# The recurrence's values brought to tokens on partitions by block transposes and on-chip transfers, and forget tiles projected ahead of them

## What is computed

```python
h = rmsnorm(x, mix_norm_g)
aq, ak, av, hq, hff, hfb, hi, hg, ga, gb = split_columns(h @ w_in)
y_attn = axial_gqa_attention(aq, ak, av, ...) @ w_branch_attn
y_hgrn = hgrn2_bidirectional(hq, hff, hfb, hi, hg, ...) @ w_branch_hgrn
# in the recurrence, per head, in chunks of tokens:
vh = heads(i, HGRN_VAL_DIM)                  # values, from the columns hi
contrib = einsum('bhnsd,bhnse->bhnde', k * exp(b_last - b), v)
o_intra = einsum('bhnts,bhnse->bhnte', scores, v)
```

## Time and profile before

| | |
|---|---|
| time, median of 3 runs | 1134.91 us (1134.86 to 1134.94) |
| the profiled execution | 1135.17 us |
| its span in the trace | 1133.4 us |
| PE busy | 1124.8 us, 99% |
| DVE busy | 628.1 us, 55% |
| ACT busy | 443.8 us, 39% |
| POOL busy | 83.3 us, 7% |
| granted PE clock | 0.998 |
| projection stage, PE units 9 to 25 | about 424 to 550 us of the span |

### The profile page before, as it was taken

The page is one execution under the profiler, slowest core; times in us unless marked ns, Lnnn a source line. Parts: engine busy times, 40 slices in busy tenths (PEclk is TensorE's granted clock), DMA queues, the critical chain, the costliest instruction groups (busy, mean ns, idle before and its releaser), DMA issues.

```text
span 1133.4 us, 16606 instructions
## 1 busy us (share of the span) xinstructions
PE 1124.8 (99%) x6359; PEld 911.9 (80%) x6359; DVE 628.1 (55%) x832; ACT 443.8 (39%) x658; POOL 83.3 (7%) x74
## 2 busy tenths in 40 slices
PE   9999999999999999999999999999999999999997
PEld 7888888888888777776788888888888888888886
DVE  6755555563333596646688767656555555542223
ACT  6423232232222544546856655544232323331223
POOL 0000000000000130000143320020000000000000
PEclk9999999999999999999999999999999999999999
DMA  6332322333322434212221212422243333332221
GB/s 199 122 111 77 108 93 93 117 104 102 102 95 74 177 109 129 75 57 84 69 92 56 71 51 92 177 96 93 79 125 120 89 121 107 119 112 93 99 88 75
DMA packets 51650, 114.78 MB, mean 101 GB/s; under 512 B 21904, under 2 KB 25104, under 8 KB 51344
## 3 DMA queue, kind: packets, MB, share of 16 engines
q1 hardware_dynamic: 32752, 105.16, 27.9%
q10 hardware_dynamic: 18848, 8.92, 2.8%
HBM read 105.41 MB, written 4.19 MB: 97 GB/s over the span
## 4 chain that ended last, share of the span: by engine, by line
PE 98%; DMA 1%; DVE 1%; ACT 0%; ACTq 0%; issue 0%; DVEq 0%
PE ps L1195 27%; PE ps L1197 27%; PE ps L1196 27%; PE ps L1221 4%; PE ps L1220 4%; PE ps L1222 4%; PE ps L1321 1%; PE ps L1338 1%; PE ps L1467 1%; PE ps L1443 1%; DMA xT<-xT_dram 0%; PE ps L1460 0%; PE ps L1421 0%; PE ps L1370 0%; DMA raw<-up_dram 0%; PE ps L1410 0%
## 5 line engine op out<-in xcount | busy, mean ns | idle before, releaser
L1195 PE MATMUL ps<-h_hi,w_hi 128*128 128x512 f32 x1024 | 407.2, 398 | 0.3 <-DVE w_lo L781 0.3
L1197 PE MATMUL ps<-h_hi,w_lo 128*128 128x512 f32 x1024 | 399.1, 390 | 0.0
L1196 PE MATMUL ps<-h_lo,w_hi 128*128 128x512 f32 x1024 | 398.7, 389 | 0.0
L781 DVE TENSOR_TENSOR w_lo<-raw,w_hi 128x1024 fp32r<-128x1024 f32 (+2 forms) x190 | 233.3, 1230 | 176.9 <-ACT w_hi L432 171.0
L432 ACT ACTIVATE w_hi<-raw 128x1024 fp32r<-128x1024 f32 (+1 forms) x182 | 194.7, 1080 | 183.8 <-PE ps L1197 71.6
L1195 PEld LDWEIGHTS ps<-h_hi,w_hi 128*128 128x128 f32 x1024 | 192.2, 188 | 55.6 <-issue 15.2
L1196 PEld LDWEIGHTS ps<-h_lo,w_hi 128*128 128x128 f32 x1024 | 192.3, 188 | 41.8 <-issue 2.9
L1197 PEld LDWEIGHTS ps<-h_hi,w_lo 128*128 128x128 f32 x1024 | 192.2, 188 | 40.4
L504 ACT ACTIVATE g_hi<-un 128x512 fp32r<-128x512 f32 (+1 forms) x44 | 27.8, 632 | 219.5 <-DVE un L781 219.5
L781 DVE TENSOR_TENSOR un<-ps,rs 128x512 f32<-128x512 f32 x44 | 30.4, 691 | 97.3 <-PE ps L1197 97.3
L1195 PE MATMUL ps<-g_hi,w_hi 128*128 128x512 f32 x176 | 68.5, 389 | 0.0
(11 more groups left out here) (232 smaller groups left out, 1151.7 us busy)
## 6 DMA issues: line engine op xcount, KB each, us to landing
raw<-up_dram SPq DMA_DIRECT2D x86, 512.0 KB, 3.3
raw<-proj_dram SPq DMA_DIRECT2D x26, 512.0 KB, 3.4
raw<-down_dram SPq DMA_DIRECT2D x16, 704.0 KB, 4.0
raw<-down_dram SPq DMA_DIRECT2D x22, 512.0 KB, 3.2
raw<-gates_dram SPq DMA_DIRECT2D x16, 512.0 KB, 3.3
raw<-branch_dram SPq DMA_DIRECT2D x8, 512.0 KB, 3.3
raw<-wout_dram SPq DMA_DIRECT2D x8, 512.0 KB, 3.2
x_spill_dram<-xT ACTq DMA_DIRECT2D x1, 2048.0 KB, 7.1
```

Source lines behind the costliest of these rows:

```text
L781: return V.tensor_tensor(out, a, b, op)
L1195: T.matmul(ps[:, bank, :], w_hi[:, slot, cols], moving_hi(j), start=start and j == 0, stop=False)
L1196: T.matmul(ps[:, bank, :], w_hi[:, slot, cols], moving_lo(j), start=False, stop=False)
L1197: ins = T.matmul(ps[:, bank, :], w_lo[:, slot, cols], moving_hi(j), start=False, stop=stop and j == tiles - 1)
```

## The change

The four value tiles of the recurrence no longer go through PE and ACT. In the list the first four forget tiles now come at items 6 to 9 and the value tiles at items 10 to 13. After DVE has copied a value tile into `v_tmp`, it transposes it in place in blocks of 32x32. SP then moves the blocks to their partitions with 16 transfers per tile (32 partitions, four pieces of 32 words each), issued before the loads of units 15, 16, 17 and 18, behind the `v_rep` transfers where these stand too. There is one `v_tmp`, so DVE waits before each further value tile until all transfers of the tile before it have landed (`vh_loaded`). The tile `av` for attention keeps its way through PE and ACT. The diff shows the list, SP ahead of the load of unit i, ACT's copy, DVE's item i, and on PE the waits of the first weighted sum and of the first contributions.

```diff
-PROJ = ([("av", 0), ("ak", 0)] + [("aq", t) for t in range(4)] + [("hi", t) for t in range(4)]
-        + [("hf", h) for h in range(4)] + [("hq", t) for t in range(4)]
+PROJ = ([("av", 0), ("ak", 0)] + [("aq", t) for t in range(4)] + [("hf", h) for h in range(4)]
+        + [("hi", t) for t in range(4)] + [("hq", t) for t in range(4)]
         + [("hf", h) for h in range(4, HH)] + [("hg", t) for t in range(4)])
-V_TILES = {i: w for w, i in enumerate(i for i, (kind, _) in enumerate(PROJ) if kind in ("av", "hi"))}
+V_TILES = {0: 0}
+HI_AT = PROJ.index(("hi", 0))
+HI_SEND = 5
...
+                        if 0 <= i - HI_AT - HI_SEND < 4:
+                            w = i - HI_AT - HI_SEND
+                            sp.wait_ge(vblk_done, w + 1)
+                            blocks = v_tmp[:].rearrange("p (t j c) -> p t j c", j=QUADS, c=BLOCK)
+                            for quad in range(QUADS):
+                                for to in range(QUADS):
+                                    sp.dma_start(v_h[BLOCK * to:BLOCK * (to + 1), :, P * w + BLOCK * quad:P * w + BLOCK * (quad + 1)],
+                                                 blocks[BLOCK * quad:BLOCK * (quad + 1), :, to, :]).then_inc(vh_loaded, 16)
                         sp.wait_ge(lo_done, BASE[name] + i + 1)
...
-                    A(v_a[:] if w == 0 else v_h[:, :, P * (w - 1):P * w], vt, ACT.Copy).then_inc(vn_done, 1)
+                    A(v_a[:], vt, ACT.Copy).then_inc(vn_done, 1)
...
-                w = V_TILES.get(i)
-                if w:
-                    dve.wait_ge(vt_done, w)
+                if kind == "hi":
+                    dve.wait_ge(*((vh_loaded, 16 * QUADS * QUADS * t) if t else (vt_done, 1)))
...
+                if kind == "hi":
+                    dve.wait_ge(proj_read, i + 1 + BANK_CREDIT)
+                    V.transpose(v_tmp[:], v_tmp[:]).then_inc(vblk_done, 1)
                 attention_step(i - FIRST_ITEM)
...
-                    pe.wait_ge(vn_done, 5)
+                    pe.wait_ge(vn_done, 1)
...
-                    pe.wait_ge(vn_done, 5)
+                    pe.wait_ge(vh_loaded, 16 * QUADS * QUADS * 4)
```

More of the change, by code:

```diff
@@ L215, in build @@
         vt_done, vn_done = sem("vt_done"), sem("vn_done")
+        vblk_done, vh_loaded = sem("vblk_done"), sem("vh_loaded")
         qsq_done, qms_done, qeps_done, qr_done = sem("qsq_done"), sem("qms_done"), sem("qeps_done"), sem("qr_done")
```

## The result

| | before | changed kernel |
|---|---|---|
| median time | 1134.93 us (4 runs, 1134.86 to 1135.34) | 1161.80 us (4 runs, 1160.60 to 1162.23) |
| profiled execution | 1135.17 us | 1160.60 us |
| its span | 1133.4 us | 1158.8 us |

The ratio is 1.0231 with a 95% interval from 1.0219 to 1.0243: slower by 2.3%, 26.9 us. The forecast was 1159.1 us, between 1154.5 and 1167.0.

What follows compares the result with a forecast made beforehand. PE's instruction stream was taken to bound the kernel, with SP's added issues deciding: 1135.2 us + 21.7 lateness + 2.5 slow clock = 1159.4, less 0.3 to the median, 1159.1 us; range 1154.5 to 1167 us.

Steps and rivals of the forecast that it cites:

- What bounds the kernel: Whole kernel: PE's instruction stream, busy 99% of the span; work removed gains its full cost, added waits are lost in full.
- The chain: Projection stage: SP's issues delay transfers, DVE's copies, ACT's exponentials, then PE's scores; 21.7 us late at `scores(5)`.
- Bounding the unseen transfer by its neighbours: SP's new issues, a shape not in the trace: 0.633 us each, from similar transfers at 0.59 to 0.63; landing 1.9 us.
- the rival with landings of 4.2 us: Second and third tiles' transfers land late, two such cost 4.6 us more: 1163.7 us and up; 10 in 100.
- The stands: PE waits before `scores(3)`, `scores(4)` and `scores(5)`, ended by ACT's exponentials: 8.4, 9.1 and 6.1 us.
- The clock term: After PE's last stand: eleven matmuls at 0.46 instead of 0.24 us, as at the kernel's start; 2.5 us, bounds 0 and 3.5.
- Late loads alone: Without DVE's wait, unit 18's load issues about 488.7 and `scores(7)` is 17 us late: 1154 us with slow clock.
- The load of unit 18 "just fits": After the fourth tile's issues: its split and exponentials end about 499.0, `scores(7)` is due at 499.1; nothing later is late.
- The rival that the issues do not bind: SP's issues in the stage all hide, needing a pitch of 0.07 us; 1.8 us gained, 1133.1 us; 5 in 100.

Runs made afterwards that it cites:

- the second trace of the changed kernel: The changed kernel, unaltered, run again beside the shortened version with useless matmuls in PE's stands: 1161.27 us, ratio 1.0229.
- the kernel with the later crowds: Against the changed kernel: four value-tile buffers, and the four groups of sixteen issues moved ahead of the loads of units 17 to 20; 1140.44 us, ratio 1.0046.
- the padded kernels: The changed kernel plus useless matmuls before the three late scores: 36, 40, 24 gave 1160.71 us; 36, 28, 16 gave 1159.38 us.
- the spread one: Against the changed kernel: four value-tile buffers, and the 64 issues placed eight ahead of each load of units 17 to 24; 1133.30 us, ratio 0.9981.

## Why the prediction was right, point by point

**What bounds the kernel: right.** Work off PE was worth its full cost once nothing made it wait (1133.30 and 1133.26 us), and every late exponential was paid in full.

**The chain: right in every link, short by 1.6 us at `scores(5)`.** On the time scale of the traces:

| step | forecast | measured |
|---|---|---|
| SP begins the first sixteen issues | 441.4 | 441.87 |
| second tile copied | 452.8 | 453.38 |
| `scores(3)` | 457.0 | 457.62 |
| third tile copied | 468.6 | 469.99 |
| `scores(4)` | 472.8 | 474.23 |
| fourth tile copied | 481.4 | 482.94 |
| `scores(5)` | 485.6 | 487.18 |
| late there | 21.7 | 23.3 |
| added behind the last stand | 2.5, all of it the clock | 2.2, of it 1.5 the clock |
| span | 1157.6 | 1158.8 |

The mis-sized term is the pitch of SP's issues. It was taken as 0.633 us; sixteen took 10.24 us, 0.64 each, which makes 0.3 us over 46 issues. And one issue of the second tile took twice as long (10.84 us for its sixteen), and the start was 0.5 us late, since the first eight `v_rep` took 6.52 us and not 5.96. The rows before already showed such long issues (0.925 us at most); I read them as an exception and left them out of the sum. Whether they are also what the runs differ by is not shown, since only the profiled run of each kernel has a trace. The forecast for the median is 2.7 us short, more than the span is: the profiled run was the fastest of four, 1.2 us below their median, where the forecast had put the median 0.3 us below it.

**Bounding the unseen transfer by its neighbours: right.** 64 issues, median 0.601 us, between `v_rep` with 0.597 and `x_tok` with 0.632. Landing had a median of 1.8 us and a maximum of 2.7; the rival with landings of 4.2 us did not come.

**The stands: lateness right, their lengths wrong.** Forecast 8.4, 9.1 and 6.1 us, 23.6 in all; measured 18.8, the three being 9.0, 6.1 and 3.8. The reason is in my own term for what follows a stand. I had said that the first two slow phases cost nothing, and for the end of the kernel that is so, since the transfers set when PE goes on. But PE is then busy longer and stands less. `scores(3)` and the unit behind it took from 457.62 to 468.2, 10.5 us instead of 6.7. DVE's waits were 12.9, 11.4 and 7.8 us instead of 8 to 11: the first began at 440.4, as soon as DVE had nothing else to do.

**The clock term: the slow clock came, and its size was met by luck.** The prediction had 2.5 us of clock and nothing else behind the last stand. The measured 8.94 - 6.74 = 2.2 us are two terms: about 1.5 us of slow clock (seven matmuls of the unit 0.43 us apart) and 0.7 us of waiting for the second exponential, which the prediction put at nothing. The 11 matmuls of its sum were those that the row of the start happens to hold, and no measure of how long the clock stays low. The sum of 2.2 us is seen again as 2.25 us in the second trace of the changed kernel and as 2.2 in the kernel with the later crowds. The Trainium skill, "TensorE: Matmul & The Clock Gate", Why this matters for your kernels, has the rule that idle gaps between bursts drop the clock; the stands of 3.8 to 9.0 us here agree with it, and so does the one of 3.2 us in the kernel with the later crowds. The two of 1.95 and 2.20 us in the padded kernels are shorter than it warns of, and PE was slow behind them too; behind one of 1.97 and one of 2.62 us it was not.

**Late loads alone: right.** The prediction gave 1154 us for the kernel without DVE's wait, "only some 5 us" less than with it; measured 1156.65, and 4.6 us less. Counting the last load only was right too: the earlier late loads hold PE up as well, but SP's queue alone sets when the last one comes. That one was issued at 489.64 (forecast 488.7), and `scores(7)` started at 495.35, 18.0 us later than in the kernel before, two periods behind 463.90 (forecast 17). The period behind it is 9.77 us, 3.0 more than 6.74, where the forecast had 2.5.

**The load of unit 18 "just fits": right.** ACT split it at 498.70 and ended the exponentials at 501.10, and `scores(7)` started at 502.86, one regular period after `scores(6)`.

**The rival that the issues do not bind** (1133.1 us, faster) was refuted for sixteen a turn, and its number is what the kernels reach that do not crowd SP: 1133.30 and 1133.26 us. The 50 ns that the prediction quotes there from the Trainium skill are given for transfers that GpSimd issues; all of these are issued by SP, at 0.60 us each. The gain that the change was after exists. It was 1.8 us, and the price for it stood on an engine with no busy time in the page.

## What to carry to other kernels

Before transfers are put on a queue, compare the issuing engine's whole turn with the period of the engine that bounds the kernel: here an issue took 0.6 us whether it carried 16 or 64 KB, so sixteen of them and the eight that stood there already made turns of 16 us against a period of 6.74, and everything queued behind them was late too. A turn somewhat too long is not yet a loss (8.3 us cost nothing here): what counts is the backlog that the turns add up to, against the slack of what is queued behind. With a buffer for each tile, spreading the same issues over more turns, or letting each carry four times as much, removed the whole cost. And when a wait is removed, look at what is next in line behind the same queue: of the 26 us lost here, the wait that the profile showed on VectorE was worth 4.6.

## What the runs showed of the hardware

An issue on SP costs 0.60 us with 128 pieces of 128 bytes and 0.63 us with 512 of them; its landing grows from 1.8 to 2.6 us. Now and then one issue takes 1.1 to 1.9 us (maximum 1192 ns in the changed kernel, 1915 ns in the spread one), without a cause that the traces show; where the issues are the critical path it adds in full (0.6 us in the changed kernel's second sixteen), and where they have slack it does not show. The 1.6 us by which the runs of the changed kernel differ may come from it, which is not shown. After stands of 1.95, 2.20 and 3.2 to 9.0 us PE's matmuls were 0.43 us apart for a while instead of 0.23, after one of 1.97 and one of 2.62 us they were not; behind the last stand this cost 1.5 us, and the period behind it grew by 2.2, since 0.7 us was a second wait that only a late PE meets. A block transpose of 128x512 costs the same 0.71 us whether its output is dense or scattered over four tiles. The granted clock read 1.00 at the very start although PE's matmuls were 0.46 us apart, while after the later stands it read 0.50 for the same kind of pace, so at the start of a trace the distance between matmuls tells more than that column.
